# Three passes of a split-float product as two: high and low activations side by side in one 512-column operand

## The reference

```
# first block: a gated linear recurrence, then attention with forgetting
h = h + hgrn2_mix(...)          # u @ a_w_in (2048 x 8192), @ a_w_out (2048 x 2048)     272 tokens
k, v, F = fox_shared_kv(...)    # @ kv_w (2048 x 4096 and 16 more columns)              272 tokens
h = h + fox_mix(...)            # @ b_w_in (2048 x 4096), @ b_w_out (2048 x 2048)       256 tokens
# second block, 256 tokens
proj = rmsnorm(x) @ w_in        # 2048 x 11264, and 16 gate columns
conv_out = centred_depthwise_conv(proj[..., :5120], conv_w, conv_b)      # 3 taps along the tokens
y_a = hyena(conv_out[..., :3072]);  y_b = mlstm(silu(conv_out[..., 3072:]), rest)
mixed = gate_a * (y_a @ w_branch_a) + gate_b * (y_b @ w_branch_b)        # 1024 x 2048 each
x = x + mixed @ w_out                                                    # 2048 x 2048
gu = rmsnorm(x) @ w_gate_up                                              # 2048 x 11264
x = x + (silu(gu[..., :5632]) * gu[..., 5632:]) @ w_down                 # 5632 x 2048
return rmsnorm(x, norm_f_w)
```

## Time and profile before

| | |
|---|---|
| median of three runs | 2994.34 us (2988.52 to 2995.01) |
| profiled execution: span | 3008.3 us; the profile gives no other time of it |
| TensorE busy, and its weight loads | 96% and 90% of the span |
| VectorE, ScalarE, GpSimd busy | 53%, 38%, 2% |
| mean granted TensorE clock | 0.938 of full |
| DMA, mean share of the 16 engines | 45% (148 GB/s over the span) |

### The profile page before, as it was taken

One profiled execution on the slowest core, in us unless ns is written; L12 is line 12 of the kernel. 1 busy time (PEld: TensorE's weight loads), 2 busy tenths in 40 slices (PEclk: granted clock), 3 DMA queues, 4 the chain that ended last, 5 costly groups with the idle time before them and its releaser, 6 DMA issues. The chain is left out here.

```text
span 3008.3 us, 53323 instructions
## 1 busy us (share of the span) xinstructions
PE 2886.8 (96%) x21514; PEld 2711.6 (90%) x21514; DVE 1579.5 (53%) x1859; ACT 1130.0 (38%) x1314; POOL 72.1 (2%) x63
## 2 busy tenths in 40 slices
PE   6999989999999989999999998889999999999998
PEld 6999987799999966799999998458999999999998
DVE  6445554556445444457665445455665555554443
ACT  4343443234334442243334444112444443443332
POOL 1000001001000000001000000000010000000000
PEclk8999985699999985699999999899999999999999
DMA  5555530054545520155555554103555555555553
GB/s 172 175 174 174 174 112 1 15 178 161 174 155 196 183 75 1 54 173 187 199 177 182 185 185 160 35 0 119 186 166 191 183 190 183 183 191 184 183 177 132
DMA packets 123687, 445.76 MB, mean 148 GB/s; under 512 B 13594, under 2 KB 15925, under 8 KB 123440
## 3 DMA queue, kind: packets, MB, share of 16 engines
q1 hardware_dynamic: 122208, 438.82, 44.5%
q0 software_dynamic: 1360, 5.27, 0.5%
HBM read 441.94 MB, written 2.10 MB: 148 GB/s over the span
## 5 line engine op out<-in xcount | busy, mean ns | idle before, releaser
L1331 PE MATMUL PS<-XH,hi 128*128 128x256 f32 (+1 forms) x5920 | 1682.4, 284 | 47.5 <-DVE lo L729 35.0
L1332 PE MATMUL PS<-XL,hi 128*128 128x256 f32 (+1 forms) x5920 | 1679.0, 284 | 0.0
L1333 PE MATMUL PS<-XH,lo 128*128 128x256 f32 (+1 forms) x5920 | 1677.6, 283 | 0.0
L729 DVE TENSOR_TENSOR lo<-raw,hi 128x1024 fp32r<-128x1024 f32 x824 | 1016.0, 1246 | 1003.3 <-ACT hi L408 992.3
L408 ACT ACTIVATE hi<-raw 128x1024 fp32r<-128x1024 f32 x824 | 863.3, 1057 | 1172.6 <-PE PS L1333 1134.9
L1331 PEld LDWEIGHTS PS<-XH,hi 128*128 128x128 f32 x5920 | 1121.8, 189 | 54.0 <-issue 33.2
L1332 PEld LDWEIGHTS PS<-XL,hi 128*128 128x128 f32 x5920 | 1121.3, 189 | 0.0
L1333 PEld LDWEIGHTS PS<-XH,lo 128*128 128x128 f32 x5920 | 1120.4, 189 | 0.0
L1331 PE MATMUL PS<-GH,hi 128*128 128x256 f32 x704 | 199.2, 283 | 0.0
L1333 PE MATMUL PS<-GH,lo 128*128 128x256 f32 x704 | 199.2, 283 | 0.0
L1332 PE MATMUL PS<-GL,hi 128*128 128x256 f32 x704 | 199.2, 283 | 0.0
(11 more groups left out here) (311 smaller groups left out, 1648.5 us busy)
## 6 DMA issues: line engine op xcount, KB each, us to landing
raw<-stream SPq DMA_DIRECT2D x828, 512.0 KB, 4.1
H<-h_in SPq DMA_DIRECT2D x4, 544.0 KB, 8.1
y_win<-windows POOLq DMA_DIRECT2D x2, 1024.0 KB, 6.0
out<-H SPq DMA_DIRECT2D x4, 512.0 KB, 3.5
dftm<-dft POOLq DMA_DIRECT2D x1, 1024.0 KB, 5.9
w<-w POOLq DMA_DIRECT2D x2, 512.0 KB, 6.4
ml_m<-mask_ml POOLq DMA_DIRECT2D x1, 512.0 KB, 4.0
a_m<-masks_a POOLq DMA_DIRECT2D x1, 272.0 KB, 7.6
```

What stands on the lines that cost most here:

```text
L729: dve.tensor_tensor(lo[s][:, :], raw[s][:, :], hi[s][:, :].bitcast(F32), ALU.subtract)\
L1331: pe.matmul(PS[:, bank, 0:n], w_hi, x_hi, start=start, stop=False)
L1332: pe.matmul(PS[:, bank, 0:n], w_hi, x_lo, start=False, stop=False)
L1333: return pe.matmul(PS[:, bank, 0:n], w_lo, x_hi, start=False, stop=stop)
```

## The change

In products over 256 tokens (600 chunks) the high and low activations become two rows of one tile (XX, or GG for the last product), and `hi` is multiplied with both at once: one matmul of 512 columns whose result fills a whole PSUM bank, `hi*XH` in its first half and `hi*XL` in its second. Then `lo*XH` (256 columns) is added into the first half. That is two matmuls and two weight loads for each weight tile in place of three and three, with the same 768 columns. Products over 272 tokens don't fit a bank twice and stay as they are, and so does the small product `gates`.

The halves have to be added when a group is read out. In most products ScalarE copies the second halves of the four banks to SBUF (`half`, 128 x 1024 elements), VectorE adds the first halves to the copy (`both_halves`), which frees the banks, and then does in place what it did before out of PSUM. In `residual` VectorE adds first the second and then the first halves to H. Functions of ScalarE and some of VectorE's work that came right behind a read-out are put off to behind chunk 5 of the group (`late`).

```diff
+        self.two = 2 * tokens <= 512
+        self.half0, self.sum0 = Product.halves, Product.sums
+        if self.two:
+            Product.sums += 2 * pairs if scaled else 0
+            if not residual:
+                Product.halves += 2 * pairs
...
-        XH = sb(ctx, "XH", [P, NT, T], F32R)
-        XL = sb(ctx, "XL", [P, NT, T], F32R)
+        XX = sb(ctx, "XX", [P, NT, 2, T], F32R)
+        XH, XL = XX[:, :, 0, :], XX[:, :, 1, :]
...
+        def bank_halves(gg):
+            return PS[:, 4 * gg:4 * gg + GROUP, SEQ:2 * SEQ]
...
                     if c == (at if then is before else 2):
                         then()
+                    if c == min(5, q.k_chunks - 1) and then is not before:
+                        late[0]()
+                        late[0] = nothing_late
...
+            def half(q, p, gg, dst):
+
+                group_done(act, q, p, gg)
+                act.activation(dst(), bank_halves(gg), ACT.Copy).then_inc(S("half_copied"), 1)
...
+            def conv_half(p, gg):
+
+                act.wait_ge(S("conv_step"), p * 24 + 12 * gg)
+                half(q, p, gg, lambda: MG[:, 2 * NT - GROUP:2 * NT, :])
+
             def silu_qk(p, gg):
-                act.wait_ge(S("conv_step"), p * 24 + (12 * gg + 12))
-                dst = QK[:, bass.ds((p - 3) * 8 + 4 * gg, 4), :]
-                act.activation(dst, dst, ACT.Silu).then_inc(S("m_qk"), 1)
+                conv_half(p, gg)
+
+                def activate():
+                    act.wait_ge(S("conv_step"), p * 24 + (12 * gg + 12))
+                    dst = QK[:, bass.ds((p - 3) * 8 + 4 * gg, 4), :]
+                    act.activation(dst, dst, ACT.Silu).then_inc(S("m_qk"), 1)
+                return activate
...
+                        both_halves(q, p, gg, tiles)
+                        t = tiles()
+                        dve.tensor_tensor(t, t, rs, ALU.mult).then_inc(S("sum_scaled"), 1)
+                    else:
+                        group_done(dve, q, p, gg)
+                        dve.tensor_tensor(tiles(), bank_group(gg, q.tokens), rs, ALU.mult).then_inc(bank_free[gg], 1)
...
+            def both_halves(q, p, gg, dst):
+
+                dve.wait_ge(S("half_copied"), 2 * p + (q.half0 + gg + 1))
+                t = dst()
+                dve.tensor_tensor(t, t, bank_group(gg, q.tokens), ALU.add).then_inc(bank_free[gg], 1)
+                dve.wait_ge(bank_free[gg], p + (q.use0[gg] + 2))
...
+                        dve.tensor_tensor(dst, dst, bank_halves(gg), ALU.add).then_inc(S("sum_scaled"), 1)
+                        dve.wait_ge(S("sum_scaled"), q.sum0 + 2 * p + gg + 1)
                     dve.tensor_tensor(dst, dst, bank_group(gg, q.tokens), ALU.add).then_inc(bank_free[gg], 1)
...
                 rest = MG[:, 2 * NT - GROUP:2 * NT, :]
 
                 def after(p, gg):
-                    group_done(dve, q, p, gg)
-                    dve.tensor_tensor(rest, bank_group(gg, SEQ),
-                                      small[:, 1, 0:SEQ].unsqueeze(1).to_broadcast([P, GROUP, SEQ]), ALU.mult)\
-                        .then_inc(bank_free[gg], 1)
-                    dve.wait_ge(bank_free[gg], p + (q.use0[gg] + 2))
+                    both_halves(q, p, gg, lambda: rest)
+                    dve.tensor_tensor(rest, rest, small[:, 1, 0:SEQ].unsqueeze(1).to_broadcast([P, GROUP, SEQ]),
+                                      ALU.mult).then_inc(S("sum_scaled"), 1)
+                    dve.wait_ge(S("sum_scaled"), 2 * p + (q.sum0 + gg + 1))
...
+            def passes_two(bank, n, w_hi, w_lo, x, start, stop):
+
+                pe.matmul(PS[:, bank, 0:2 * n], w_hi, x, start=start, stop=stop, skip_group_check=True)
+                return pe.matmul(PS[:, bank, 0:n], w_lo, x[:, 0], start=False, stop=stop, skip_group_check=True)
...
-                                    ins = passes(4 * gg + j, q.tokens, hi[s][:, col], lo[s][:, col],
-                                                 xh[:, x, 0:q.tokens], xl[:, x, 0:q.tokens],
-                                                 k == 0, k == 2 * q.k_chunks - 1)
+                                    ins = (passes_two if q.two else passes)(
+                                        4 * gg + j, q.tokens, hi[s][:, col], lo[s][:, col],
+                                        xx[:, x, :, 0:q.tokens], k == 0, k == 2 * q.k_chunks - 1)
...
-            product(prod["down"], GH, GL, pieces=("gl_ready", 0, 4))
+            product(prod["down"], GG, pieces=("gl_ready", 0, 4))
```

More of the change, by code:

```diff
@@ L68, with __init__ @@
     uses = [0, 0]
[L70 removed]
+    halves = 0
+    sums = 0
+    def __init__(self, pairs, k_chunks, tok0, tokens, x_tile=0, residual=False, scaled=True):
         self.c0, self.pairs, self.k_chunks = Product.chunks, pairs, k_chunks
@@ L102, in layout @@
 def layout():
-    Product.chunks, Product.uses = 0, [0, 0]
+    Product.chunks, Product.uses, Product.halves, Product.sums = 0, [0, 0], 0, 0
     p = {}
@@ L109, in layout @@
     p["b_in"] = Product(4, 8, META, SEQ)
-    p["b_out"] = Product(2, 8, 0, SEQ)
+    p["b_out"] = Product(2, 8, 0, SEQ, residual=True)
     p["w2"] = Product(11, 8, 0, SEQ)
     p["gates"] = Mini(0, SEQ)
-    p["br_b"] = Product(2, 4, 0, SEQ)
-    p["br_a"] = Product(2, 4, 0, SEQ, x_tile=HT)
-    p["out2"] = Product(2, 8, 0, SEQ)
+    p["br_b"] = Product(2, 4, 0, SEQ, scaled=False)
+    p["br_a"] = Product(2, 4, 0, SEQ, x_tile=HT, scaled=False)
+    p["out2"] = Product(2, 8, 0, SEQ, residual=True)
     p["gate_up"] = Product(11, 8, 0, SEQ)
-    p["down"] = Product(2, 22, 0, SEQ)
+    p["down"] = Product(2, 22, 0, SEQ, residual=True)
     return p
@@ L252, in program @@
             w3_t = (w3_0, w3_1)
+            with ExitStack() as sub:
+                br_t = [sb(sub, f"br_t{s}", [P, GROUP, SEQ]) for s in range(2)]
         with ExitStack() as ph:
@@ L299, in group, with nothing_late, do, both @@
                         then()
+                    if c == min(5, q.k_chunks - 1) and then is not before:
+                        late[0]()
+                        late[0] = nothing_late
+            def nothing_late():
+                pass
+            late = [nothing_late]
+            def do(after, p, gg):
+                late[0] = after(p, gg) or nothing_late
+            def both(after, p, gg):
+                (after(p, gg) or nothing_late)()
             then, p0 = before, 0
@@ L305, in follow @@
                     mid()
-                group(p0, 1, lambda: after(p0, 0))
+                group(p0, 1, lambda: do(after, p0, 0))
                 if pairs == 2:
-                    group(p0 + 1, 0, lambda: after(p0, 1))
-                    group(p0 + 1, 1, lambda: after(p0 + 1, 0))
+                    group(p0 + 1, 0, lambda: do(after, p0, 1))
+                    group(p0 + 1, 1, lambda: do(after, p0 + 1, 0))
                 elif pairs > 2:
                     with eng.Fori(p0 + 1, p0 + pairs) as p:
-                        group(p, 0, lambda: after(p - 1, 1))
-                        group(p, 1, lambda: after(p, 0))
+                        group(p, 0, lambda: do(after, p - 1, 1))
+                        group(p, 1, lambda: do(after, p, 0))
                 p0 += pairs
-                then = (lambda last, do: lambda: do(last, 1))(p0 - 1, after)
+                then = (lambda last, of: lambda: both(of, last, 1))(p0 - 1, after)
             return then
@@ L548, in _ @@
             tail_b = follow(act, q, chunk, lambda: scaled_input("b_in", (2, None), BN, META, SEQ),
-                            [(2, nothing), (2, through(q, BZ, 2, ACT.Silu, "b_act"))], b_mid, at=1)
+                            [(2, halves(q, BQ, 0)), (2, through(q, BZ, 2, ACT.Silu, "b_act"))], b_mid, at=1)
             def b_mix():
@@ L661, in mixers, with branch_half, after, first_branch_half @@
                     act.activation(XH[:, 4 * k:4 * k + 4, 0:SEQ], src, ACT.Copy).then_inc(S("xh_ready"), 1)
-            follow(act, prod["br_b"], chunk, mixers, [(2, nothing)], at=3, early={2: tail_w2})
+            def branch_half(q):
+                def after(p, gg):
+                    act.wait_ge(S("branch_taken"), q.half0 - prod["br_b"].half0 + 2 * p + gg - 1)
+                    half(q, p, gg, lambda: br_t[gg][:, :, :])
+                return after
+            def first_branch_half(q):
+                def after(p, gg):
+                    if p == 0:
+                        half(q, p, gg, lambda: br_t[gg][:, :, :])
+                    else:
+                        branch_half(q)(p, gg)
+                return after
+            tail_br = follow(act, prod["br_b"], chunk, mixers, [(2, first_branch_half(prod["br_b"]))], at=3,
+                             early={2: tail_w2})
             def mixed_piece(k):
@@ L671, in mixed_group @@
             def mixed_group(p, gg):
+                branch_half(prod["br_a"])(p, gg)
                 if p == 0:
                     mixed_piece(gg)
-            follow(act, prod["br_a"], chunk, lambda: None, [(2, mixed_group)])
```

(2 more changed lines are left out.)

106 lines of the change are left out of this document (66 added, 40 removed).

## The result

The changed kernel took 3011.01 us (median of 7 runs, 3000.97 to 3012.08), the kernel before 2992.63 (7 runs) beside it: a ratio of 1.0048, 95% interval 1.0035 to 1.0062. That is slower by 14 us by the ratio and by 18 by the medians, where 69 us less were forecast. The profiled execution of the changed kernel has a span of 3003.0 us.

A forecast was written before the change was run, and what follows sets the result against it. TensorE was taken to set the pace within the products. On a span of 3008.3 us, -96 + 17 + 3 + 3.8 + 2.3 + 0.7 = -69 us, scaled to the median: 2926 us, 8-in-10 range 2885 to 3000.

The forecast's parts named there:

- The gain on TensorE: 256-column products: the pair costs 333.3 ns, 20.1 less than the triple, over 4800 triples 96 us saved.
- then a 512-column matmul costs 213.3 + 2.2 = 215.5 ns: Wide matmul on TensorE: its columns at 2.4 GHz plus the 2.2 ns fixed cost read from plain float32 rows.
- The reading of the excess: 256-column matmuls on TensorE: the other 9 ns of excess is a weight load only just hidden under a 107 ns stream.
- Rival 1: TensorE: the excess is per matmul, 11.1 ns, however wide; gain 53 us, time 2966 us; chance 0.27.
- rival 2: TensorE: excess scales with columns or shrinks only 2.2 ns; gain 0 to 10.6 us, 3006 to 3017 us; chance 0.17.
- rival 3: TensorE: the load beneath the `lo` matmul is no longer late; pair 324.4 ns, 139 us gained, 2884 us; chance 0.14.
- The read-outs: Added copies and additions: w2 stalls 17 us, clock 3, ends of products 3.8, behind b_in 2.3, out2 0.7.
- the stalls: w2's ten convolved groups, TensorE waiting for `lo` 3: 2.66 us in four loop groups, 1.88 in others; 17 us net.
- The wait behind b_out: End of b_out: a second addition lengthens TensorE's wait from 2.67 to 3.9 us.
- The clock: w2: four loop stalls of 2.66 us may drop the clock to 1.2 GHz; 0 to 6 us, taken as 3.
- Behind b_in: End of b_in: copy and addition come in front of ScalarE's squares, which TensorE waits for; 2.3 us.
- the mixers behind `gates`: Behind w2: the two chunks of `gates`, 5.6 us, hide the read-out's 2.3 us, so nothing is added.

The follow-up runs named there:

- m1: Matmuls alone, computing nothing of the reference, varying type, width and traffic: 512 adjacent float32r columns 226.8 ns, two rows 272 apart 233.3, bfloat16 215.9.
- m2: Matmuls alone, nothing of the reference, varying the operand's start and stride: 512 float32r columns 226.7 to 233.3 ns, 256 columns 116.7 to 123.2.
- e4: Changed kernel, w2 read-outs behind chunk 3, put-off functions put off at seams too, both parts adjacent in 256-column stages, tiles 544 elements apart: 2988.35 us.
- e6: As e4, but tiles 576 elements apart, low part of 272-column stages moved, a scratch tensor cut: 2985.79 us, ratio 0.9974.
- m3: Matmuls alone, nothing of the reference, with fewer weight columns and rows, more starts, and pairs at tiles 576 apart: pair 353.3 ns from element 0, 346.7 from 8.
- e7: Kernel before, with only XH and XL laid as the two rows of one tile XX: 3015.2 us, ratio 1.0064.
- e1: Changed kernel with the 512-column matmul cut back into two of 256, layout and read-outs kept: 3043.44 us, ratio 1.0161 to the kernel before.
- e8: As e6, but every row starts 8 elements later: 2973.58 us, ratio 0.9939 to the kernel before.

## Why the prediction was wrong

- **The gain on TensorE failed**: -96 us forecast, -32 measured for the operand, and +21 for the layout, which wasn't priced at all. The step that failed is "then a 512-column matmul costs 213.3 + 2.2 = 215.5 ns". In the kernel it costs 231.7. Of the 16 ns between, 11 are float32r's: it has 13.4 ns per matmul by itself where plain float32 and bfloat16 have 2.6 (m1, m2). The other 5 aren't shown: m1 puts 6.5 on the place of the second row, but e4 and e6, which have no gap between the rows, have dearer pairs in `gate_up`, and in `down`, whose rows are adjacent too, the 512-column matmul of after takes 230.2 (its `lo` 116.7).
- **The reading of the excess** as a weight load only just hidden was a guess to make two kinds of rows agree. m3 has 512 columns over a quarter of the weight load at 231.7 ns, so it doesn't explain the excess there; at 256 columns, where it was guessed, narrower weights take 6.4 of 13.3 ns off. The change of type between the two kinds of rows stood in the forecast's own sentence and wasn't priced. Nor was the place, though a row had it: the window of 118.5 ns in the earlier trace rows holds both `gate_up`, at 117.6, and `down`, at 120.0, where the operand's rows start at multiples of 256.
- **Rival 1 had the mechanism, rival 2 the time.** The excess is fixed per matmul, so one of three goes, whole in `down` and half in `gate_up`; but there the layout takes 3.7 ns back, and the pair gains 2.9 ns on the triple, under the 5 ns at which rival 2 was to decide. Rival 2's 3006 to 3017 us held the time, for a reason that it doesn't give: luck. (The stated range was also said to take in all but the tail of rival 3, whose 2884 us lies just outside its 2885.)
- **The read-outs were right in sum, in part by luck**: 26.8 us forecast (17 + 3 + 3.8 + 2.3 + 0.7), 29 measured (e7 to e1). At the pace of e1's triples the stalls are 14.2 us instead of 17 and the clock some 7 instead of 3. In the w2 of after the ten stalls are where they were said to be. From start to start, less the usual step, the four in the loops hold TensorE up by 2.2 to 2.3 us (2.66 forecast) and five of the others by 1.5 (1.88): three chunks of 8 x 349 ns are 8.4 us where 8.0 were reckoned, so each has 0.4 more cover. The last QK group, 3.65, was underrated: the Silu at the seam was overlooked. Together 20.3 us, where 21.9 were forecast. The wait behind b_out, 3.92, was forecast as 3.9.
- **The clock** was forecast at 3 us for four stalls near the longer wait. In after it stayed at 1.00 behind three of them and fell to 0.50 behind the fourth, a wait of 2.05 us of the same kind, and behind the last QK group's 3.49. Each step's excess over the usual one, added up, gives 1.4 and 1.0 us. After, behind the stall of 1.39, behind that of 2.05 and behind that of 3.49:

```profile
1374.00:1376.00 2.00, 1.25 (x7) 1.00 0.06 20
1450.40:1452.40 2.00, 2.00 (x8) 0.50 1.00 285
1597.40:1599.40 2.00, 1.94 (x6) 0.50 0.41 131
```

- **Behind b_in** the mixer grew by 4.7 us, not 2.3, and the mixers behind `gates`, put at nothing, by 2.6. The copy and addition come in front of the Silu there, and 1.5 and 1.0 of it appear in e7 already, with no new read-out. out2 has no stall; 0.7 was forecast.
- **What isn't placed**: summed over all stretches behind a_in's mixer, the trace of after is 8 us longer than that of before, against 14 by the ratio and 18 by the medians. 4.6 of the difference may be `down`, which has either of two values; the rest isn't placed.

## What to carry to other kernels

A fixed cost per instruction is read from rows of the same data type; where none exists, the bounds must be argued as wide as the types can differ, and a small kernel with the very sequence in question is the better guide: the alternating pairs of m1 and m3 gave the 350, 353 and 347 ns of `gate_up` in after, e6 and e8, their parts did not, and neither gave every stage. Merging operands into one tile is itself a change: price the new addresses apart from the saved instructions, for instance by laying out the old kernel that way. And where a read-out grows by two steps, first move it behind the chunk that it makes late: that took 17 us off w2 here, and some 25 off the median.

## What the runs showed of the hardware that was not expected

- float32r matmuls cost 13.5 ns over their columns at 512 and 13.3 at 384 and 256 (from element 0), but bfloat16 2.6, with the same weights' shape and no other traffic; at 128 columns the distance was 111.4 ns for 53.3 of columns.
- The moving operand's start matters by a few ns: 113.5 (element 48), 116.7 (8), 120.0 (0), 123.2 (1) at 256 columns. Many distances are a multiple of 3.33 ns: 226.7, 230.0, 233.3; 346.7, 350.0, 353.3. One program showed 346.7 and 353.3 ns for the same pair in two stages of one execution (e6).
- DMA, VectorE and ScalarE beside the matmuls cost them nothing: 233.3 ns with and without.
- 96 matmuls over only 32 weight rows ran at the 1.2 GHz level though TensorE never paused; stretches of m3 (PE, PEld, DVE, ACT and POOL busy, PEclk), in them and some 30 us later:

```profile
175.00:205.00 30.00, 30.00 (x72) 23.13 (x71) 0.00 (x0) 0.00 (x0) 0.00 (x0) 0.50 0.00 1
...
240.00:250.00 10.00, 10.00 (x44) 8.03 (x44) 0.00 (x0) 0.00 (x0) 0.00 (x0) 1.00 0.00 0
```
